# Third gate projection of a streaming encoder layer as Strassen block products, with its sums on GpSimd and VectorE

## The reference, cut to what matters

```
h = rmsnorm(x, p["g_attn"])
proj = h @ p["w_in"]
g_logit = proj[..., o5:]                       # 3 gates, D columns each
gates = jax.nn.sigmoid(g_logit).reshape(b_, l_, N_BRANCHES, D_MODEL)
merged = gates[..., 0, :] * br_a + gates[..., 1, :] * br_b + gates[..., 2, :] * br_c
x = x + merged @ p["w_out"]
x = x + hierarchical_moe(rmsnorm(x, p["g_ffn"]), p)
```

## Time and profile before

| | |
|---|---|
| median of 3 runs | 635.23 us (634.72 to 637.25) |
| profiled execution | 637.16 us, its span 635.3 us |
| TensorE busy (matmuls) | 611.6 us, 96% of the span |
| VectorE, ScalarE, GpSimd busy | 291.2, 186.6, 148.7 us |
| chain that ended last | TensorE 91%, VectorE 3%, DMA 2% |
| HBM read | 147.12 MB |

### The profile page before, as it was taken

One profiled execution on the slowest core, in us unless ns is written; L12 is line 12 of the kernel. 1 busy time (PEld: TensorE's weight loads), 2 busy tenths in 40 slices (PEclk: granted clock), 3 DMA queues, 4 the chain that ended last, 5 costly groups with the idle time before them and its releaser, 6 DMA issues.

```text
span 635.3 us, 9981 instructions
## 1 busy us (share of the span) xinstructions
PE 611.6 (96%) x3746; PEld 378.6 (60%) x3746; DVE 291.2 (46%) x813; ACT 186.6 (29%) x582; POOL 148.7 (23%) x341
## 2 busy tenths in 40 slices
PE   8999999999999999999999999999999999978895
PEld 7888867677456667666677767854443444333341
DVE  3343947757883589772043321685123133132112
ACT  5534224532478445423100101211221221111111
POOL 1596627733584525510000000000000000000000
PEclk9999999999899999999999999999999999989899
DMA  8893553212301343323589990099999999999993
GB/s 285 193 292 113 191 171 100 68 67 85 113 2 33 117 150 100 100 67 100 150 251 401 406 387 24 14 411 401 421 419 420 420 419 419 421 419 419 422 391 98
DMA packets 57715, 150.57 MB, mean 237 GB/s; under 512 B 12352, under 2 KB 40448, under 8 KB 45760
## 3 DMA queue, kind: packets, MB, share of 16 engines
q1 hardware_dynamic: 57664, 149.89, 63.4%
HBM read 147.12 MB, written 2.76 MB: 236 GB/s over the span
## 4 chain that ended last, share of the span: by engine, by line
PE 91%; DVE 3%; DMA 2%; issue 2%; ACT 1%; SPq 0%; DVEq 0%
PE PS L832 28%; PE PS L842 21%; PE PS L1229 10%; PE PS L1123 7%; PE PS L1268 6%; PE PS L1258 5%; PE PS L958 2%; PE PS L915 2%; PE PS L1180 2%; PE PS L983 2%; PE PS L825 1%; PE PS L1025 1%; PE PS L966 1%; DMA W<-in_w_in 1%; PE PS L904 1%
## 5 line engine op out<-in xcount | busy, mean ns | idle before, releaser
L832 PE MATMUL PS<-hT,W 128*128 128x320 f32 x416 | 117.2, 435 | 0.0
L832 PEld LDWEIGHTS PS<-hT,W 128*128 128x128 f32 x416 | 77.5, 190 | 33.4 <-issue 3.8
L1229 PE MATMUL PS<-E,xT 128*32 128x256 f32 (+1 forms) x1088 | 64.5, 390 | 7.7 <-issue 7.4
L1229 PEld LDWEIGHTS PS<-E,xT 128*32 128x32 f32 x1088 | 35.5, 112 | 36.1 <-issue 16.2
L2206 POOL TENSOR_SCALAR means<-sums 128x4 f32<-128x4 f32 (+3 forms) x35 | 7.3, 210 | 188.6 <-ACT junk L1368 187.6
L1123 PE MATMUL PS<-h,S 128*128 128x512 f32 (+1 forms) x96 | 48.2, 625 | 0.3 <-DVE S L1996 0.3
L842 PE MATMUL PS<-W,hT 128*128 128x256 f32 (+5 forms) x256 | 41.7, 353 | 0.0
L1268 PE MATMUL PS<-yb,WG 128*128 128x512 f32 (+1 forms) x96 | 38.5, 609 | 0.8 <-DVE yb L2121 0.8
L842 PEld LDWEIGHTS PS<-W,hT 128*128 128x128 f32 (+1 forms) x256 | 31.5, 163 | 8.4 <-issue 1.3
L842 PE MATMUL PS<-W,mergedT 128*128 128x384 f32 (+3 forms) x192 | 35.7, 381 | 0.0
L832 PE MATMUL PS<-uT,W 128*128 128x320 f32 x128 | 34.6, 432 | 0.0
(11 more groups left out here) (316 smaller groups left out, 985.3 us busy)
## 6 DMA issues: line engine op xcount, KB each, us to landing
E<-in_w_e SPq DMA_DIRECT2D x93, 1024.0 KB, 22.3
W<-in_w_in SPq DMA_DIRECT2D x7, 1536.0 KB, 7.2
W<-in_w_in SPq DMA_DIRECT2D x7, 1024.0 KB, 8.0
W<-in_w_mem_kv SPq DMA_DIRECT2D x4, 1024.0 KB, 6.9
W<-in_w_glu SPq DMA_DIRECT2D x4, 768.0 KB, 7.5
W<-in_w_out SPq DMA_DIRECT2D x2, 1536.0 KB, 14.8
X<-in_x_prompt SPq DMA_DIRECT2D x4, 512.0 KB, 4.8
W<-in_w_o_mem SPq DMA_DIRECT2D x1, 1536.0 KB, 6.7
```

The source lines that it names most:

```text
L832: ins = mm(out[:, 0:TOK], w[:, k, cols:cols + 128], rhs[:, k, :], start=(k == 0), stop=(k == kt - 1))
L1229: ins = mm(PS[r:r + B, AB, 128 * which.start:128 * which.stop], xT[:, k, place_ + B * n:place_ + B * n + B], E13[slot][:, which, k, j::2], ...
```

## The change

Only gateA is computed in another way. Its 8 feature blocks are taken in 4 pairs. The weights of a pair (8 input slices x 256 outputs) are cut into four blocks: input half (slices 0 to 3, 4 to 7) by output block, a11, a12, a21, a22 in the program's names (a12 and a21 are the second input half of the first and the first input half of the second output block). The tokens are cut into halves of 160 and input halves, b11 to b22. The result of a pair, two blocks by two token halves, comes from seven block products in place of eight, each with four products of 160 columns. For them are needed:

- four sums of the input, sumT [128, 4, 4, 160], made once on GpSimd (`token_sums`), behind GpSimd's part of step gateB 2;
- per pair two sums of weight blocks, s1 and s2, kept in the unused end of the slot, and a third written over a21 (`weight_sums`, GpSimd, behind gateB 5, gateB 7, part b of pair 0 and part c of pair 1); and a fourth over a12 on VectorE, after part a;
- additions of the product blocks to each other on VectorE, straight from PSUM into gateA (`gate`), after which ScalarE does the tanh of the whole pair in one instruction of 640 columns.

Each pair is three units in the ring, a (three products), b and c (two each), emptied by VectorE; TensorE waits for x_sums and early_sums before the third product of a, and for late_sums before the second of c. The planner puts a, b and c as fills by their work in place of one fill per slot. gateA's weights come in four chunks of 256 columns instead of three (384, 384, 256), so the slots of outB, glu and wout change places. sumT lies where X0 and later X lie, so qT moves elsewhere and the loads of X wait for the last part of gateA; on SyncE's queue, grow, the stores of the final states and the first glu chunk stand behind them, as before.

```diff
+GATE_PAIRS = KD // 2
+GATES = [("gateA", m) for m in range(GATE_PAIRS)]
+HALF = TOK // 2
...
-over_d("gateA", KD, 128, (0, 2, 1))
-over_d("outB", 4, 128, (0, 2))
-over_d("glu", 4, 256, (1, 0, 2))
-over_d("wout", KD, 128, (1, 0, 2))
+over_d("gateA", KD, 128, (0, 2, 1, 0))
+over_d("outB", 4, 128, (2, 1))
+over_d("glu", 4, 256, (0, 2, 1))
+over_d("wout", KD, 128, (0, 2, 1))
...
+GATE_WORK = {"a": 3.2, "b": 2.2, "c": 2.2}
+FILL = 4.3
+def work_of(step):
+    return GATE_WORK[step[2]] if step[0] == "gateA" else WORK.get(step[0], 0.5)
...
+    def fill_up():
+        nonlocal room
+        room += FILL
+        while fills and room >= work_of(fills[0]) / 2:
+            room -= work_of(fills[0])
+            fill()
...
-    fills = [("gateB", d) for d in range(KD)] + [("gateA", d) for d in range(KD)]
-    held, pace, due = False, LATE_PACE, spent
-    attention("mla", MLA_UNITS, 1)
-    fill(1)
+    fills = [("gateB", d) for d in range(KD)] + [("gateA", m, part) for m in range(GATE_PAIRS) for part in "abc"]
+    held, pace, due, room = False, LATE_PACE, spent, 0.0
+    attention("mla", MLA_UNITS)
...
-    return "dve" if unit[0].startswith("out") else "act"
+    return "dve" if unit[0].startswith(("out", "gateA")) else "act"
...
-        (qT,), _ = place(at0, ("qT", [128, H, TOK]))
+        (sumT,), sum_end = place(at0, ("sumT", [128, 4, KD // 2, HALF]))
...
+        (qT,), qT_end = place(at5, ("qT", [128, H, TOK]))
...
+        def gate_blocks(name):
+            slot = W[SLOT_OF[CHUNK_NO[name]]]
+            w = chunk_view(name)
+            s1, s2 = (slot[:, 2048 + 512 * n:2560 + 512 * n].rearrange("p (k n) -> p k n", k=KD // 2) for n in range(2))
+            lo, hi = slice(0, KD // 2), slice(KD // 2, KD)
+            return w[:, lo, 0:128], w[:, hi, 0:128], w[:, lo, 128:256], w[:, hi, 128:256], s1, s2
+        tokens = [[hT[:, 4 * r:4 * r + 4, HALF * c:HALF * c + HALF] for c in range(2)] for r in range(2)]
...
-            sp.wait_ge(s["psum_full"], UNIT_NO["mla", "S", len(MLA_UNITS) - 1] + 1)
+            sp.wait_ge(s["psum_full"], UNIT_NO["gateA", GATE_PAIRS - 1, "c"] + 1)
             for t, (f, n) in enumerate(TILES):
                 sp.dma_start(X[0:n, t, :], xp[f:f + n, :] if t < 2 else xs).then_inc(s["x_again"], 16)
...
+            def gate(kind, m, part):
+                no = GATES.index((kind, m))
+                use(f"{kind}{m}")
+                a11, a12, a21, a22, s1, s2 = gate_blocks(f"{kind}{m}")
+                (b11, _), (b21, b22) = tokens
+                out = begin((kind, m, part))
+                def product(n, lhs, rhs):
+                    for k in range(KD // 2):
+                        ins = mm(out[:, HALF * n:HALF * n + HALF], lhs[:, k, :], rhs[:, k, :], start=(k == 0), stop=(k == KD // 2 - 1))
+                    return ins
+                if part == "a":
+                    product(0, a11, b11)
+                    product(1, a12, b21)
+                    pe.wait_ge(s["x_sums"], 4)
+                    pe.wait_ge(s["early_sums"], no + 1)
+                    end(product(2, s2, sumT[:, 1]))
+                elif part == "b":
+                    product(0, s1, sumT[:, 0])
+                    end(product(1, a21, sumT[:, 2]))
+                else:
+                    product(1, a22, sumT[:, 3])
+                    pe.wait_ge(s["late_sums"], no + 1)
+                    end(product(0, a12, b22))
...
+                elif kind == "gateA":
+                    m, part = which
+                    if part == "c":
+                        act.wait_ge(*emptied_at(UNIT_NO[kind, m, "c"]))
+                        z = gateA[:, 2 * m:2 * m + 2, :]
+                        fn(z, z, ACT.Tanh, scale=0.5).then_inc(s["gates_made"], 1)
                 elif kind.startswith("gate"):
-                    if (kind, which[0]) == ("gateA", 0):
-                        act.wait_ge(s["stored"], 16 * 10)
-                    dst = {"A": gateA, "B": gateB, "C": mergedT}[kind[-1]]
-                    empty(dst[:, which[0], :], full((kind, which[0]))[:, 0:TOK], ACT.Tanh, scale=0.5)
+                    empty({"B": gateB, "C": mergedT}[kind[-1]][:, which[0], :], full((kind, which[0]))[:, 0:TOK], ACT.Tanh, scale=0.5)
...
+            joined = {}
+            def gate(kind, m, part):
+                z = gateA[:, 2 * m:2 * m + 2, :].rearrange("p d n -> p (d n)").rearrange("p (b n) -> p b n", b=4)
+                src = full((kind, m, part))[:, 0:3 * HALF].rearrange("p (b n) -> p b n", b=3)
+                if part == "a":
+                    _, a12, _, _, _, s2 = gate_blocks(f"{kind}{m}")
+                    link(V_.tensor_copy(z[:, 3], src[:, 0]))
+                    joined["a"] = st.mark(V_.tensor_tensor(z[:, 0::3], z[:, 3:4].broadcast_to([128, 2, HALF]), src[:, 1:3], ALU.add),
+                                          s["emptied_dve"])
+                    V_.tensor_tensor(a12, a12, s2, ALU.subtract).then_inc(s["late_sums"], 1)
+                elif part == "b":
+                    st.after(joined["a"])
+                    link(V_.tensor_tensor(z[:, 1:3], z[:, 3:4].broadcast_to([128, 2, HALF]), src[:, 0:2], ALU.add))
+                    joined["b"] = st.mark(V_.tensor_tensor(z[:, 3], z[:, 2], src[:, 0], ALU.add), s["emptied_dve"])
+                else:
+                    st.after(joined["b"])
+                    st.mark(V_.tensor_tensor(z[:, 1:3], z[:, 1:3], src[:, 0:2], ALU.add), s["emptied_dve"])
...
-                    dve.wait_ge(*emptied_at(UNIT_NO["gateA", KD - 1]))
+                    dve.wait_ge(s["gates_made"], len(GATES))
...
+            def token_sums():
+                for g in range(2):
+                    pool.wait_ge(*emptied_at(UNIT_NO["xT", NT - 1, g]))
+                (b11, b12), (b21, b22) = tokens
+                t1, t2, t3, t4 = (sumT[:, n] for n in range(4))
+                first = st.mark(tt(t1, b12, b11, ALU.subtract), s["x_sums"])
+                st.mark(tt(t3, b22, b12, ALU.subtract), s["x_sums"])
+                st.after(first)
+                link(tt(t2, b22, t1, ALU.subtract), s["x_sums"])
+                st.mark(tt(t4, b21, t2, ALU.subtract), s["x_sums"])
+            def weight_sums(no):
+                name = "{}{}".format(*GATES[no])
+                pool.wait_ge(*chunk_loaded_at(name))
+                a11, a12, a21, a22, s1, s2 = gate_blocks(name)
+                link(tt(s1, a21, a22, ALU.add))
+                link(tt(s2, s1, a11, ALU.subtract))
+                tt(a21, a11, a21, ALU.subtract).then_inc(s["early_sums"], 1)
+            sums_at = {("gateB", 2): token_sums}
+            for no, step in enumerate((("gateB", 5), ("gateB", KD - 1), ("gateA", 0, "b"), ("gateA", 1, "c"))):
+                sums_at[step] = lambda no=no: weight_sums(no)
...
+                if (kind, *which) in sums_at:
+                    sums_at[kind, *which]()
```

37 lines of the change are left out of this document (24 added, 13 removed).

## The result

The changed kernel takes **645.46 us** (median of 6 runs, 641.96 to 646.59) where the kernel before takes 636.16 us (6 runs, 634.72 to 637.70): a ratio of **1.0137, 95% interval 1.0117 to 1.0156**. It is slower, as forecast, but by 9 us and not by 3.5, and above the range. A second set of runs of the same pair gave 644.51 us against 636.10 us, 1.0119 (1.0095 to 1.0142).

A forecast was written before the change was run, and what follows sets the result against it. TensorE bounds up to the last output projection, then the expert weight stream. -4.1 + 2.6 + 0.4 + 2.5 + 2.1 = +3.5 us on 635.23 gave 638.7 us; 1 in 10 below 632.5, 1 in 10 above 643.0.

The forecast's parts named there:

- The gain: gateA on TensorE: 34.5 us of products removed, 30.4 us of 160-column products added, 4.1 us saved, 2.5 at least.
- the last rival: gateA's products: each part pays a start, twelve parts instead of eight, 0.1 us each, 0.4 us; no chance of its own.
- GpSimd's operations: Added sums on GpSimd: 1.1 us for a weight sum of 512 elements, 1.4 us for a token sum of 640.
- VectorE beside them: VectorE operations with both inputs in SBUF alternate with GpSimd's sums, each sum costing VectorE its own length.
- The constant stretch of 0.30 us: Alternative to the full block: each VectorE operation beside GpSimd loses 0.30 us; six lose 1.8 us, first wait nil.
- First wait: TensorE at gateB block 5, VectorE delayed by token sums: 2.6 us (0 to 3.5); block 6 adds 0.4 (0 to 0.8).
- Second wait: TensorE at gateA pair 1 part a, for the bank of the last scores: 2.5 us, between 1.1 and 4.4.
- Third wait: TensorE waits 2.1 us (0 to 3) for output weights, as moved loads and stores delay SyncE's queue by 3.6 us.
- the room of the second output chunk, 1.8 us: Output projection: wout1 landed at 373.2 us and was needed at 375.0, leaving 1.8 us before any wait.
- The clock: Rival, chance 0.17: new waits halve TensorE's clock at two places, 1.65 us each, 3.3 us more, 642.0 us.
- The expert stage "one to one": The expert stage runs at the weight stream's speed, so front gains or losses move the end by the same amount.
- the larger waits: Upper end of the forecast's own range: waits of 3.5, 0.8, 4.4 and 3 with a gain of 2.5: +9 us.

The follow-up runs named there:

- token_early: The changed kernel with the four token sums on GpSimd moved from behind the tables of turn 12 to behind those of turn 11: 640.06 us.
- pair2_late: The changed kernel with GpSimd's three weight sums of gateA pair 2 held until VectorE's back-turn of turn 15 is done: 641.60 us.
- x_late_before: The kernel before with only the loads of X, and what queues behind them, waiting for the last block of gateA: 641.94 us.
- expert_ahead_before: The kernel before with the first expert's weights issued ahead of X on SyncE's queue: 637.05 us, ratio 1.0008.
- expert_ahead: The changed kernel with the first expert's weights (3 MB) issued ahead of X on SyncE's queue, instead of behind the router weights: 639.60 us.
- after_again: The changed kernel run and profiled once more without an edit, the second set of runs: 644.51 us, ratio 1.0119 to the kernel before.

## Why the prediction was wrong in size

The sum was +3.5 us on the span; it came out as +8.2: +3.9 at gateB, +0.1 at gateA, +4.9 from outB to the router, -0.7 behind.

- **The gain, forecast 4.1 us: right.** 0.1356 us from start to start against the 0.136 that I took, and 3.84 us in all. The 0.26 us that are missing are less than the 0.4 us that the last rival put on the starts of the parts.
- **GpSimd's operations, taken as 1.1 and 1.4 us: too short.** Undisturbed they take 1.26 and 1.53 us. The slope from the tables (2.2 ns per element more) was right and gave 1.3 and 1.6 us; I took values between these and the 1.0 and 1.2 us of the faster 256-element form. The Trainium skill (GPSIMD Engine Reference, Elementwise — side-by-side cycle accounting), scaled down from 2048 elements, gave 1.12 and 1.41 us; the measurement decides against scaling through zero.
- **VectorE beside them: right.** Three back-turn operations became 1.83, 1.82 and 1.82 us. The constant stretch of 0.30 us that I had weighed against it is out. The Trainium skill (SBUF — State Buffer, Who interferes with whom) says that the pair of ports that the two share is an exclusive lock. The trace agrees: from start to start a VectorE operation took 1.75 us in place of 0.40 beside a sum of 1.53 us, and 1.47 us beside one of 1.26 us, so each lost some 0.2 us less than the length of GpSimd's undisturbed operation.
- **First wait, 2.6 + 0.4 us: right place, 3.9 us in all.** Block 5 waited 1.9 us (forecast 2.6, with a slip in it: 4.2 less 0.69 us is 3.5, not 3.7), block 6 0.6, and block 7, which I had not looked at, 1.1. The step that failed is that the delay ends with the next bank. VectorE was busy for 28.5 of the 31 us up to block 5 in the kernel before, so it could not catch up: token_early shows that without the first delay the other two waits nearly go, and pair2_late that they go as well when TensorE itself comes later. The room ahead of block 6, which I had counted as free, had been used up.
- **Second wait, 2.5 us at pair 1 part a: 1.6 us there in the second profile (none in the first, where the fall of the clock took its place), but 2.0 us one part earlier that the text did not have.** The step that failed is the list of banks: in a ring of five, part c of pair 0 needs the bank of part a of the same pair, whose join stands behind the back-turn of turn 14, and pair 2's sums stretched that by 3.1 us (282.30 to 286.66 for three operations that take 1.22 in pair2_late). The 1.0 us for late_sums came in the second profile. Together 4.6 us there (5.3 by the stretches: 44.56 - 43.15 + 3.84); in the first profile 4.0 (43.29 - 43.15 + 3.84).
- **Third wait, 2.1 us: 4.9 us.** Two steps failed. The queue slipped by 5.8 us (first expert load 13.4 us after gateA's end, before 7.6), not by the 3.6 us of the moved issues: the router load held the queue 3.63 us in place of 1.48. x_late_before shows that the late group of loads does this (3.38 us there). That it is X in flight just ahead is likely, but not shown: in expert_ahead_before, with X nearly at its old place and the expert's 3 MB ahead of it, the same load held the queue 4.01 us. From SyncE's timeline of the changed kernel:

```profile
321.84 0.82 SPq L715 DMA_DIRECT2D X<-in_x_prompt  x2
...
327.41 3.63 SPq L738 DMA_DIRECT2D wr<-in_w_re  x1
...
335.48 0.90 SPq L726 DMA_DIRECT2D E<-in_w_e  x2
...
357.76 0.43 SPq L649 DMA_DIRECT2D W<-in_w_out  x1
```

  And I took the room of the second output chunk, 1.8 us; the first was the one that came late. Before, it was issued at 348.50 us and took 17.9 us, so it landed 3.4 us ahead of 369.84:

```profile
348.50 0.38 SPq L615 DMA_DIRECT2D W<-in_w_out  x1
W<-in_w_out SPq DMA_DIRECT2D x1, 1536.0 KB, 17.9
```

  With that room and the 3.6 us of the issues the wait would have come out at 0.2 us, so the two mistakes pulled against each other. Against TensorE the chunk was issued 5.3 us later and took 1.2 us more. From the chain of waits of the changed kernel:

```profile
357.76 19.07 DMA W<-in_w_out
```

  It landed at 376.83 us, and TensorE began at 376.88, when glu had ended 34.46 us after 339.31 (as long as from 335.38 to 369.84 before), at 373.8: a wait of 3.1 us, and 1.8 us of the clock behind it (20.89 us for what took 19.10).
- **The clock, a rival at 0.17, two places at 1.65 us: half right.** At the output projection it fell in all five profiled executions that had one wait of 2.7 us and more there, and cost 1.7 to 1.8 us. Near 289 us it fell in one profile of two and cost nothing, since TensorE was not what the next step waited for. It cost nothing behind gateB's first wait in pair2_late either, but at pair 1 part a of expert_ahead it did: its 1.7 us took the place of the next wait of 1.0 us, and gateA is 0.5 us longer than in after_again.
- **The expert stage "one to one": nearly.** The last stretch is 0.7 and 1.4 us shorter in the two profiles of the changed kernel, up to 2.1 shorter in the kernels made from it, and 2.2 longer in x_late_before. No run here says why.
- **The range.** The larger waits, taken together, had given +9 us; I then expected at most +7 and set the upper end at 643.0 us. The measured time lies with the larger waits, for the reasons above.

So each mechanism of the forecast was there. The two waits behind GpSimd's sums were cut off too early, at the first consumer I had looked up, and the third rested on too small a slip of the queue.

## What to carry to other kernels

Before handing elementwise work to GpSimd, price it on every VectorE operation with both inputs in SBUF that it will meet (here 1.35 us for a sum of 1.53 us and 1.07 us for one of 1.26 us), and follow the delay through all later consumers until VectorE has an idle stretch as long; where VectorE has such a stretch, let it do the work itself (0.7 us for 512 elements here, against 1.07 of blocking; whether the idle stretch or the engine decides stayed open). A load that must wait longer takes everything behind it in its queue along: list for each later load the room between landing and need, put a load that is allowed earlier into the gap, and hold GpSimd's work by a semaphore where its place matters, since its order in the program does not.

## What had not been expected of the hardware

- Beside GpSimd's sums VectorE operations that take one tensor were stretched too: a GELU TENSOR_SCALAR of 320 elements took 1.42 us (0.32 in the changed kernel, 298.62 us) and a COPY of 4 elements 1.12 us (0.17 there). From VectorE's timeline of pair2_late, and of after_again:

```profile
293.68 1.42 DVE L1961 TENSOR_SCALAR gelu<-gelu 128x320 f32<-128x320 f32 x1
```

```profile
296.92 1.12 DVE L1849 COPY finals<-hS 128x4 f32<-128x4 f32 x1
```

  So were scans, 1.69 and 1.29 us for 0.68 and 0.33. From VectorE's timeline of the changed kernel, turn 13:

```profile
267.46 1.69 DVE L1832 TENSOR_TENSOR_SCAN rotB<-s5tmp,rotA 128x256 f32<-128x256 f32 x1
...
269.08 1.29 DVE L1832 TENSOR_TENSOR_SCAN rotB<-s5tmp,s5par,rotA 128x64 f32<-128x64 f32 x1
```

- A clock at half speed for 3.4 us cost nothing where TensorE had 1.6 us to wait anyway, and the next wait of 1.0 us was spared as well; the same fall at the output projection cost 1.8 us.
- The issue of one and the same router load took SyncE's queue 1.48 us in the kernel before, behind a glu chunk alone. It took 2.7 to 3.6 us in the six profiles with X just ahead of that chunk, and 3.9 to 4.8 us in the seven with the expert's 3 MB ahead, one of them with X at its place of before. What in the stream decides it no run parts.
